# Two transformer blocks on one core: a first norm whose rows come by a product, larger and turned weight rings, and seven moved steps

## The reference

```
h = layernorm(x, ln_in_g, ln_in_b)
for layer in 0, 1:
    proj = h @ w_in[layer]       # A: 4 differential heads, B: 4 forgetting heads, C: 4 stick-breaking heads
    y    = concat(A * silu(ag), B * silu(bg), C * silu(cg))          # 8 chunks of 128
    h    = layernorm(ALPHA * h + y @ w_out[layer], ln_g, ln_b)
h2 = rms_norm(h) ; proj = h2 @ w_in_2
    # X: attention over the 128 best keys that an indexer (I, 8 heads) picks, with a bias table
    # HGRN2: 4 heads of a chunked linear recurrence
    # M: 4 heads of latent attention with rope
mixed = sum over the three branches of sigmoid(gate) * (branch @ w_up)
x = h + mixed @ w_out_2
x = x + (silu(n @ w_gate) * (n @ w_up)) @ w_down,  n = rms_norm(x)
out = rms_norm(x)
```

## Time and profile before

| | |
|---|---|
| three runs | 1962.64 us median (1958.49, 1962.64, 1964.73) |
| the profiled execution, its time | 1960.21 us |
| its span, mean granted clock of PE | 1958.4 us, 0.940 |
| busy PE, DVE, ACT, POOL | 1747.6, 866.7, 801.5, 590.6 us |
| HBM read, written | 138.00 MB, 10.49 MB |

### The profile page before, as it was taken

The page is one execution under the profiler, slowest core; times in us unless marked ns, Lnnn a source line. Parts: engine busy times, 40 slices in busy tenths (PEclk is TensorE's granted clock), DMA queues, the critical chain, the costliest instruction groups (busy, mean ns, idle before and its releaser), DMA issues. The chain is left out here.

```text
span 1958.4 us, 20995 instructions
## 1 busy us (share of the span) xinstructions
PE 1747.6 (89%) x7742; PEld 1325.8 (68%) x7742; DVE 866.7 (44%) x1478; ACT 801.5 (41%) x1512; POOL 590.6 (30%) x291
## 2 busy tenths in 40 slices
PE   4899998889999987898989898978779989999997
PEld 3666765567667655675655675767658778888786
DVE  4353344553533445452895656465417313211402
ACT  2244446522344465323324555555443334443411
POOL 4332222134322121322211222222046435444540
PEclk9998999899989998998989998989889989999999
DMA  6312212033122120323112222322155333333221
GB/s 179 92 44 65 65 44 65 12 86 87 46 65 57 51 75 12 87 81 87 32 46 65 60 70 60 113 60 74 39 168 187 86 95 97 97 96 99 77 97 43
DMA packets 204116, 149.85 MB, mean 77 GB/s; under 512 B 14956, under 2 KB 183536, under 8 KB 204016
## 3 DMA queue, kind: packets, MB, share of 16 engines
q1 hardware_dynamic: 199488, 133.57, 24.1%
q0 software_dynamic: 4528, 14.95, 2.4%
HBM read 138.00 MB, written 10.49 MB: 76 GB/s over the span
## 5 line engine op out<-in xcount | busy, mean ns | idle before, releaser
L1422 POOL TENSOR_TENSOR weights_rounded<-weights_raw,weights_rounded 128x1024 fp32r<-128x1024 f32 (+1 forms) x237 | 562.9, 2392 | 1153.1 <-ACT weights_rounded L1952 1152.8
L1488 PE MATMUL proj<-hT_high,weights_rounded 128*128 128x512 f32 (+1 forms) x1904 | 643.0, 409 | 35.7 <-POOL weights_rounded L1422 20.4
L1488 PEld LDWEIGHTS proj<-hT_high,weights_rounded 128*128 128x128 f32 x1904 | 370.1, 195 | 126.2 <-issue 39.0
L1488 PE MATMUL proj<-hT_low,weights_rounded 128*128 128x512 f32 (+1 forms) x952 | 379.1, 398 | 0.0
L1952 ACT ACTIVATE weights_rounded<-weights_raw 128x1024 fp32r<-128x1024 f32 (+1 forms) x237 | 233.6, 1009 | 140.2 <-DMA weights_raw<-in_w_ffn_down 58.7
L1484 PE MATMUL proj<-weights_rounded,hT_high 128*128 128x512 f32 (+1 forms) x640 | 209.3, 405 | 40.7 <-DVE hT_low L2033 15.8
L1488 PEld LDWEIGHTS proj<-hT_low,weights_rounded 128*128 128x128 f32 x952 | 185.7, 195 | 40.4 <-issue 5.3
L1484 PEld LDWEIGHTS proj<-weights_rounded,hT_high 128*128 128x128 f32 x640 | 125.9, 200 | 71.6 <-issue 32.2
L1611 PE MATMUL score<-qk 64*128 64x256 f32 (+3 forms) x256 | 79.6, 496 | 28.4 <-DVE logits L2201 15.2
L1654 PE MATMUL attn_out<-probs_T,V 128*64 128x128 f32 (+1 forms) x560 | 89.2, 294 | 0.0
L1640 PE MATMUL turned_probs<-constants,probs 128*128 128x128 f32 x320 | 61.0, 291 | 22.7 <-ACT probs_T L1842 22.5
(11 more groups left out here) (463 smaller groups left out, 2794.1 us busy)
## 6 DMA issues: line engine op xcount, KB each, us to landing
weights_raw<-in_w_in SPq DMA_DIRECT2D x113, 512.0 KB, 4.1
weights_raw<-in_w_out SPq DMA_DIRECT2D x24, 512.0 KB, 3.8
weights_raw<-in_w_ffn_gate SPq DMA_DIRECT2D x22, 512.0 KB, 3.9
weights_raw<-in_w_ffn_up SPq DMA_DIRECT2D x22, 512.0 KB, 3.8
weights_raw<-in_w_ffn_down SPq DMA_DIRECT2D x22, 512.0 KB, 3.6
gates<-constants POOLq DMA_DIRECT2D x24, 256.0 KB, 2.7
weights_raw<-gates SPq DMA_DIRECT2D x24, 256.0 KB, 4.9
weights_raw<-in_w_in SPq DMA_DIRECT2D x20, 256.0 KB, 3.2
```

The source lines that it names most:

```text
L1422: nc.gpsimd.tensor_tensor(piece_view(WR, p, "raw"), piece_view(WF, p, "raw"), piece_view(WR, p, "high"), ALU.subtract).then_inc(w_low, 1)
L1488: mm = nc.tensor.matmul(ps[:, on], w_[:, c0:c0 + P], x_[:, k, on], start=first, stop=last)
```

## The change

- **Start**: four weight pieces are issued right behind the first tile of x, the other tiles behind them; the norm's two rows go to one partition each, by ACT's queue, with the identity. PE spreads them to 128 partitions by four products with a row of ones into banks 3 to 6, and DVE reads them there, in halves. The transposes of a tile stand ahead of the norm of the next but one, the splits of the first two pieces ahead of the first transposes. The rest of the constants waits for the spread.
- **Rings**: RINGS_1 has 8 raw slots (7 before) and 7 high ones as before, two in place of three in the pool and five in place of four in the bias table's space. RINGS_FRONT and RINGS_TAIL begin at other slots. The bias table's small matrix moves to the gate logs' space.
- **Rope**: the first rotation job has weight 0 in place of 1, the next 1.6 in place of 1.1.
- **Bias groups**: two to a tick while the items of tile 3 run.
- **y**: chunks 0 to 4 are split right behind the last gate's group, chunk 5 where all six stood.
- **wo**: tile 2 also begins ahead of the last ticks, with one tick between tiles 1 and 2.
- **HGRN**: a gate projection stands between turn and state, one fewer at the end of the head; in the last head both ticks stand behind `hgrn_out`.
- **Tail**: the pieces of the gates that are left over no longer wait for `tail`; the pieces of the `up` groups still do.

```diff
-IN_POOL, IN_BIAS = [SLOT * i for i in range(POOL_SLOTS)], [BIAS_AT + SLOT * i for i in range(4)]
-RINGS_1 = IN_POOL[0:7], IN_POOL[7:10] + IN_BIAS
-RINGS_FRONT = IN_POOL[0:5], IN_POOL[5:10]
+IN_POOL, IN_BIAS = [SLOT * i for i in range(POOL_SLOTS)], [BIAS_AT + SLOT * i for i in range(5)]
+RINGS_1 = IN_POOL[0:8], IN_POOL[8:10] + IN_BIAS
+RINGS_FRONT = IN_POOL[4:5] + IN_POOL[0:4], IN_POOL[9:10] + IN_POOL[5:9]
...
-RINGS_TAIL = [PIECE * i for i in range(TAIL_RING)], [PIECE * (TAIL_RING + i) for i in range(TAIL_RING)]
+RINGS_TAIL = ([PIECE * i for i in (5, 6, 7, 8, 0, 1, 2, 3, 4)],
+              [PIECE * (TAIL_RING + i) for i in (2, 3, 4, 5, 6, 7, 8, 0, 1)])
...
-        if state["bias"] < len(tables) and n < len(items) and items[n]["kind"] == "I":
+        for _ in range(2 if n < len(items) and items[n]["tile"] == NT - 1 else 1):
+            if state["bias"] == len(tables) or n >= len(items) or items[n]["kind"] != "I":
+                break
...
-    steps.extend([("ln_in", 0), ("ln_in", 1)])
+    steps.append(("ln_in", 0))
+    turn_rows(0)
+    steps.append(("ln_in", 1))
     open_values(0)
-    turn_rows(0)
     for t in range(NT):
         value_tiles(0, t)
         if t + 1 < NT:
+            turn_rows(t + 1)
             if t + 2 < NT:
                 steps.append(("ln_in", t + 2))
-            turn_rows(t + 1)
...
-            jobs += [(lambda h=h: rope_raw(h, 0), 1, 0), (lambda h=h: rope_two(h), 1.1, 0),
+            jobs += [(lambda h=h: rope_raw(h, 0), int(h > 1), 0), (lambda h=h: rope_two(h), 1.1 + 0.5 * (h == 1), 0),
...
+            if c == 5:
+                for k in range(5):
+                    steps.append(("split_x", ("y", k, 1)))
             steps.append(("gate2", g))
...
-        for c in range(6):
-            steps.append(("split_x", ("y", c, 1)))
+        steps.append(("split_x", ("y", 5, 1)))
...
-        late.append(group("T", wo, N=512, K=KD, tile=1, dst=("resid", 0), src="y", layer=l, late=True))
-        steps.append(("half", late[1]))
-        groups[late[1]]["cut"] = 6
+        for t in (1, 2):
+            late.append(group("T", wo, N=512, K=KD, tile=t, dst=("resid", 0), src="y", layer=l, late=True))
+            steps.append(("half", late[t]))
+            groups[late[t]]["cut"] = 6
+            if t == 1:
+                tick()
...
+        if p["free_raw"] < 0:
+            seq = max(p["free_high"], slabs[p["slab"]]["first"] - 3) if i > 3 else -1 if i < 2 else 1
...
         jobs.append((lambda h=h: hgrn_turn(h), 1))
+        jobs.append((next_gate, 0))
         jobs.append((lambda h=h: hgrn_state(h), 1))
-        jobs.append((next_gate, int(last)))
-        jobs.append((lambda h=h: hgrn_out(h), int(last)))
+        if not last:
+            jobs.append((next_gate, 0))
+        jobs.append((lambda h=h: hgrn_out(h), 2 * last))
         if not last:
             jobs.append((next_gate, 0))
         jobs.append((lambda h=h: hgrn_meansq(h), int(last)))
-        if not last:
-            jobs.append((next_gate, 0))
...
-    state["after"] = ("tail", 0)
     steps.append(("tail", 0))
...
     new_rings(RINGS_TAIL)
+    state["after"] = ("tail", 0)
...
             for i, p in enumerate(pieces):
-                if i in (2, 4):
-                    tile_in(i // 2 + 1)
+                if i == 4:
+                    for t in range(1, NT):
+                        tile_in(t)
                 if i == len(RINGS_1[0]):
+                    sp.wait_ge(rows_spread, 1)
                     constants_in()
...
+            pe.wait_ge(first_rows_in, 32)
+            pe.wait_ge(ones_set, 1)
+            for i, b in enumerate(down[PROJ_BANKS:PROJ_BANKS + 4]):
+                mm = nc.tensor.matmul(b[:, :], z[0:1, 0:P], rows[0:1, i // 2, S * (i % 2):S * (i % 2) + S], start=True, stop=True)
+            mm.then_inc(rows_spread, 1)
...
+            act.dma_start(rows[0:1, 0, :], a["ln_in_g"].partition_broadcast(1)).then_inc(first_rows_in, 16)
+            act.dma_start(rows[0:1, 1, :], a["ln_in_b"].partition_broadcast(1)).then_inc(first_rows_in, 16)
+            act.dma_start(CN[:, 0:P], a["constants"][:, 0:P]).then_inc(ident_in, 16)
...
+                if not rows_need:
+                    dve.wait_ge(rows_spread, 1)
+                    gain, shift = down[PROJ_BANKS:PROJ_BANKS + 2], down[PROJ_BANKS + 2:PROJ_BANKS + 4]
+                    for i in range(2):
+                        half = slice(S * i, S * i + S)
+                        ins = nc.vector.scalar_tensor_tensor(h_tok[:, t, half], src[:, half], mv[:, 0:1], gain[i][:, :],
+                                                             ALU.subtract, ALU.mult)
```

More of the change, by code:

```diff
@@ L239, in plan @@
     stages = [("scores", 0), ("soft1", 0), ("soft2", 1), ("soft3", 2), ("trans", 3), ("pv", 4)]
-    state = dict(lo=0, n=0, fin=0, rings=RINGS_1, raw=0, high=0, after=("ln_in", 1), bias=0, squared=None, mid=None,
+    state = dict(lo=0, n=0, fin=0, rings=RINGS_1, raw=0, high=0, after=("ln_in", 0), bias=0, squared=None, mid=None,
                  rounds=[])
@@ L466, in plan @@
         steps.extend(("group", g) for g in late)
-        wide_tiles(wo, (2, 3), dst=("resid", 0), src="y", layer=l)
+        wide_tiles(wo, (3,), dst=("resid", 0), src="y", layer=l)
         wo = slab("wo", wide=True, cols=512, layer=l, half=1)
@@ L559, in place_splits @@
         seq = max(p["free_high"], min(p["free_raw"] + 2, slabs[p["slab"]]["first"] - 2))
+        if p["free_raw"] < 0:
+            seq = max(p["free_high"], slabs[p["slab"]]["first"] - 3) if i > 3 else -1 if i < 2 else 1
         assert seq < slabs[p["slab"]]["first"]
         k = max(at.get(seq, -1), start[p["after"]], before)
-        while steps[k + 1][0] not in ("group", "half", "early", "down"):
+        while i > 3 and steps[k + 1][0] not in ("group", "half", "early", "down"):
             k += 1
@@ L1103, in two_blocks @@
         table_row = L[0:4, 0, 0:2 * P]
-        circulant = bias[:, 3, OFF[3]:OFF[4]].rearrange("p (h n) -> p h n", h=4)
+        circulant = gate_e[:, :].rearrange("p (h n) -> p h n", h=4)
         table_out = nc.dram_tensor("bias_table", (4, 2 * P), F32, kind="Internal").ap()
@@ L1340, in _ @@
             tile_in(0)
-            sp.dma_start(rows[:, 0, :], a["ln_in_g"].partition_broadcast(P)).then_inc(first_rows_in, 16)
-            sp.dma_start(rows[:, 1, :], a["ln_in_b"].partition_broadcast(P)).then_inc(first_rows_in, 16)
-            sp.dma_start(CN[:, 0:P], a["constants"][:, 0:P]).then_inc(ident_in, 16)
-            tile_in(1)
             for i, p in enumerate(pieces):
-                if i in (2, 4):
-                    tile_in(i // 2 + 1)
+                if i == 4:
+                    for t in range(1, NT):
+                        tile_in(t)
                 if i == len(RINGS_1[0]):
+                    sp.wait_ge(rows_spread, 1)
                     constants_in()
@@ L1988, in _ @@
             nc.vector.memset(struck_out, NEG).then_inc(eps_set, 1)
+            nc.vector.memset(z[0:1, 0:P], 1.0).then_inc(ones_set, 1)
             dve.wait_ge(eps_set, 4)
@@ L1997, in layernorm @@
                 dve.wait_ge(var_done, nth)
-                if rows_need:
-                    dve.wait_ge(rows_in, rows_need)
-                else:
-                    dve.wait_ge(first_rows_in, 32)
+                if not rows_need:
[5 more added lines that the diff above has]
+                                                             ALU.subtract, ALU.mult)
+                    link(ins)
+                    dve.wait_ge(rstd_done, nth)
+                    for i in range(2):
+                        half = slice(S * i, S * i + S)
+                        ins = nc.vector.scalar_tensor_tensor(h_tok[:, t, half], h_tok[:, t, half], lnv[:, 1:2],
+                                                             shift[i][:, :], ALU.mult, ALU.add)
+                    ins.then_inc(ln_done, 1)
+                    return
+                dve.wait_ge(rows_in, rows_need)
                 link(nc.vector.scalar_tensor_tensor(h_tok[:, t, :], src, mv[:, 0:1], rows[:, 0, :], ALU.subtract, ALU.mult))
```

3 lines of the change are left out of this document (2 added, 1 removed).

## The result

The changed kernel takes 1904.57 us (median of 4 runs, 1901.75 to 1907.93), the kernel before beside it 1961.46. The ratio is 0.971, with a 95% interval of 0.9687 to 0.9733: 57 us faster. The forecast was 1868, 92 faster; the time lies inside the whole range (1836 to 1906), 1.4 us under its upper end, and outside the forecast's own (1850 to 1885). The profiled execution took 1907.93 us.

A forecast was written before the change was run, and what follows sets the result against it. PE was taken to bound the kernel, through its idle time and the half clock behind its waits, with DVE setting the pace in the search. Eight terms summed to 91.9 us off 1960.2, giving 1868, whole range 1836 to 1906.

The forecast's parts named there:

- the forecast's case: Whole kernel: the summed terms give 1868 us, with its own range 1850 to 1885 and a chance of 0.55.
- Small change only: Rival, chance 0.08: rows land late, high ring still holds `wo` and search, gates' buffers hold HGRN; 1910 us.
- the gates' copies: Rival, chance 0.18: in HGRN, waits on gate buffers replace the state waits; HGRN gives 2, not 22; 1888 us.
- wo term: Output weight: two waits, 3.8 and 3.5 us, go with 3.2 of clock as loads stop waiting; -10.5 us.
- The start: Kernel's start: first product earlier, at about 20.8 us, and shorter waits for later tiles' transposes; -7 us (-14 to +2).
- the clock comes back less than the waits do: Sign of failure, whole kernel: less half-clock time regained than waiting time; no size given.
- L1422 waits anywhere else: Sign of failure: late weight pieces showing as PE waits on this line at other places; no size given.
- rope and the pair in C: Attention layers: waits behind rotations go, -3 us; two successive items after the last gate no longer pair, -15.8 us.
- y: Before `wo`: earlier splits replace the 5.1 us wait by about 1.5 at chunk 0 and 2.5 at chunk 5; -7.6.
- HGRN: HGRN: state waits of 16.4 us and 15.4 of clock go, 2.5 a head given back to gate copies; -22.
- the tail: Tail: waits of 12.7 and 3.39 us go with their clock, a late `up` slab costs 4.5; -16 us.
- the search: Second block through top-k search: 2.5 us earlier start, 7.5 shorter because DVE bounds it; -10 us (-21 to -5).

The follow-up runs named there:

- e5: The changed kernel with the start's steps, issues, spread and norm of the kernel before; 1910.58 us, ratio 0.9744.
- e9: The kernel before with only the new weights of the rotation jobs; 1971.25 us, ratio 1.0063.
- e1: The changed kernel with all six splits of y together again behind the last gate; 1904.45 us, ratio 0.9709.
- e2: The changed kernel with y's chunk 5 split right behind the gate's last multiplication; 1895.76 us, ratio 0.9677.
- e6: The changed kernel with the rotation jobs' old weights, 1 and 1.1; 1886.85 us, ratio 0.9627.
- e3: The changed kernel with HGRN's jobs in the order of before; 1921.57 us, ratio 0.9794.
- e4: The changed kernel with the tail's old rings and the old place from which splits wait for `tail`; 1914.84 us, ratio 0.9763.
- e12: The changed kernel with e6's and e2's edits, and the last gate projected behind the first `up` group; 1887.42 us, ratio 0.9629.
- e8: The kernel of e2 with only a quarter of each branch gate stored and read back four times; 1889.28 us, ratio 0.9638.
- e11: The changed kernel with one bias group to a tick, as before; 1904.80 us, ratio 0.9721.
- e7: The kernel of e2 with splits of the first-loaded pieces five groups ahead of use, not three; 1904.07 us, ratio 0.9711.

## Why the prediction was partly right

**The number.** 1904.6 is inside the whole range, but the 57 us are not those of the forecast's case. The nearest case was the rival *Small change only*, 1910 with a chance of 0.08. Its reasons did not come true either: the rows did not land late, the `wo` waits did go, and the gates' copies did not take the state waits' place. Misses of several terms, the largest of them with the wrong sign, happened to stop short of the bound: that the range held is luck in part.

**Right.** The kernel got faster by removing PE's idle time and the half clock behind it, and the bound is still PE. The spread's price (7.05 forecast, 7.20 measured), the wo term's mechanism (the waits of 3.8 and 3.4 on L1422 are gone; the second was 3.44, not the 3.5 of the prediction) and the new pair at items 2 and 3 (3.4 forecast, 3.39 measured) hold; the wait at chunk 0 came, at 2.26 and not 1.5. The start gave 9.1 in its stage where 7 was forecast, since the rows were there 2.7 us sooner; by e5 it is worth 7. The rings and `wo` were not undone by themselves.

**The clock, over all.** The prediction counted some 38 us of clock: 1.4 (start), 0.8 (rope), 4.8 (C), 5.4 (y), 3.2 (wo), 2.6 (search), 15.4 (HGRN) and 4.2 (tail). PE's busy time fell by 6.6 us with the spread's 7.2 in it, so about 14 came. Two of the prediction's own signs of failing came: "the clock comes back less than the waits do", and late pieces in "L1422 waits anywhere else".

**Wrong: rope and the pair in C.** The prediction had -3 and -15.8; e9 measures +12 for the same edit alone. The step that failed is "Items of C keep the same work between them, so nothing else becomes late". A tick taken out of a pair is a tick fewer before the next fixed point, here the last gate and y. Part of what the pair's wait gave, the wait before y took (5.10 to 6.96). The rest of the price is clock: PE's idle time in e9 is 1.9 us less than before, its busy time 11.7 more, most of it in one stretch a layer behind y. The prediction took "2 x 2.4 of clock" as gained with the wait, and the opposite came. These two terms are some 31 us off, where the whole forecast was 35 too far. No rival named them: the prediction weighed each pair against its own neighbours only. The misses below don't add up to what is left of the 35, since y's is partly this one again and the start's goes the other way.

**Wrong: y.** Forecast -7.6, measured 0 in this company, give or take 6 (e1). The step is "Five of the splits move ahead of the gate's exponential ... by which chunk 5 comes later on ACT's queue", with 2.5 us at chunk 5. The wait was 4.54, and e2 shows that it came from DVE's queue. That is partly the same error again: with the old weights (e6) the wait is 1.55. With them the stages that hold C, y and wo give 12.6 and 9.1, 21.7 in all, where y and wo alone were forecast at 18.1. What y's early splits are worth with the old weights wasn't measured apart.

**Mis-sized: HGRN.** Forecast -22; 13.3 by its stage (about 17 with the same matmuls), 16 by e3. The mechanism held: the state waits went and the bank's wait came. Given back was a little more than the 2.5 a head that I took: L1503 <- L1797 rose from 4.7 to 13.2 and a wait of 3.8 on the same copy came at L1595, 12.3 in all where 10 was forecast. The stage's idle time fell from 43.6 to 32.7 us, by more than these lines show. The term mis-sized is the clock: all of the 15.4 was counted as gained. Cut into stretches of some 10 us, each weighed by one less its granted clock, the stage sums to 30.1 us before and 22.1 after: 8 were gained, since new waits have slow stretches of their own.

**Mis-sized: the tail.** Forecast -16; 10.8 by its stage (about 7 with the same matmuls), 10 by e4. The term is "about 4.5 us after PE could use it": it measured 7.58. The prediction had not seen the transfer that holds the gate's copy, but by e12 and e8 that is at most a part; the rest stays open. Of the clock, 4.2 forecast, the same sum gives 2.3.

**Mis-sized: the search.** Forecast -10; 7.9 by its stages. The 7.7 on L1422 did go. The other part, "7.5 shorter, because DVE bounds it", was nothing (e11): the stretch took 83.5 us where "about 75 us long" was expected.

A rough sum by what was measured, with terms that overlap in part: 9 (start) + 21.7 (y and wo without the weights' edit) + 8 + 13 to 16 + 11 to 14.6, less 12 for the weights, is 51 to 57.

## What to carry to other kernels

When a schedule is written by a running credit, an edit of one weight moves every later step: simulate the whole order and look at what stands at each fixed point (a gate, a split, a barrier), not at the pairs that change. The list of waits is not enough to judge it by: with the new weights the waits got no longer, and PE's busy time did. Undo each part of a bundle by itself; here one part of eight cost 12 to 16 us and hid inside a gain of 57. And of the half clock behind a wait count only what no new wait will bring back.

## What the runs showed of the hardware

**DVE beside POOL.** The subtraction of 128x512 took 0.62 us and, begun at 342.53 in the changed kernel while POOL's 341.71 to 344.05 ran, 2.07: it ended 0.55 us after POOL did. In e2, with no split of POOL beside it, it took 0.69. The operations that read a PSUM operand stay at 0.69 in the same stretch (341.92). The Trainium skill (SBUF — State Buffer, SBUF: two separate sides) says that a DVE operation with two SBUF inputs and a GpSimd operation that reads SBUF exclude each other for a whole instruction, and the trace agrees. e7 adds that DVE doesn't get in between the splits of a row: its operation, begun at 67.75 in the third of seven, ended at 78.97, behind the seventh.

**The start's clock.** The granted clock reads 1.00 over the first product's stretch in both kernels, while its first matmuls take 0.63 us, as at 0.50, and only later ones 0.39. So the column can't be read there. The spread's 7.20 us of busy PE did not change that: the products behind it began as slowly as before. PE was idle for 3.11 us between the two. The rule of the Trainium skill that was weighed in the prediction (TensorE: Matmul & The Clock Gate, What's actually happening), by which activity releases the clock, gave no gain here; with that idle time between, no run here can decide it.

**The clock behind short waits.** In e9 the granted clock was 0.50 for 17.0 us behind waits of 0.92 and 1.38 us, while PE was busy for 16.34 of them; in the kernel before it was 0.50 for 6.8 us behind one of 1.40.

**A transfer's landing.** A store of 256 KB landed 2.6 us after its issue in the median of 24 (e2), one of 64 KB 2.2 (e8). Single ones took up to 6.4 and 7.7.
